# Two steps reordered on VectorE: a scaling in a band attention, and the joining of rotated pairs in an attention weave

## The reference

```
def apply_rotary(x, cos, sin):
    x1, x2 = jnp.split(x, 2, axis=-1)
    return jnp.concatenate([x1 * c - x2 * s, x1 * s + x2 * c], axis=-1)
...
b_out = moba_attention(rot(mq), rot(mk), heads(mv))
```

```
m = jnp.maximum(jnp.max(scores, axis=-1, keepdims=True), sink_b)
e = jnp.exp(scores - m)
probs = e / (jnp.sum(e, axis=-1, keepdims=True) + jnp.exp(sink_b - m))
out = jnp.einsum('bnhgqk,bnkhd->bnqhgd', probs.astype(v.dtype), vb)
```

## Time and profile before

| | |
|---|---|
| time, median of 3 runs | 2084.06 us (2082.97 to 2089.34) |
| the profiled execution | 2090.52 us, span 2088.5 us |
| PE busy | 2051.5 us, 98% of the span |
| PE weight loads busy | 1383.0 us, 66% |
| DVE busy | 987.6 us, 47% |
| ACT busy | 546.9 us, 26% |
| POOL busy | 29.6 us, 1% |
| chain that ended last | PE 89%, DVE 4%, ACT 4%, issue 2%, DMA 1% |

### The profile page before, as it was taken

The page is one execution under the profiler, slowest core; times in us unless marked ns, Lnnn a source line. Parts: engine busy times, 40 slices in busy tenths (PEclk is TensorE's granted clock), DMA queues, the critical chain, the costliest instruction groups (busy, mean ns, idle before and its releaser), DMA issues.

```text
span 2088.5 us, 23656 instructions
## 1 busy us (share of the span) xinstructions
PE 2051.5 (98%) x9752; PEld 1383.0 (66%) x9752; DVE 987.6 (47%) x1457; ACT 546.9 (26%) x1078; POOL 29.6 (1%) x16
## 2 busy tenths in 40 slices
PE   9999999999999999999999999999999999999998
PEld 5677565876888777786678888868754444333357
DVE  3776544556655454674566657644541101101145
ACT  4745352320001232203222435330140000000024
POOL 0121000000000000000000000000000000000000
PEclk9999999999999999999999999999999999999999
DMA  8311111322222120223221211312659999999961
GB/s 212 81 41 49 57 58 41 81 101 78 84 81 91 46 76 31 81 81 68 85 81 41 81 41 41 81 52 81 242 206 397 416 405 419 420 419 420 419 240 41
DMA packets 117978, 316.79 MB, mean 152 GB/s; under 512 B 38064, under 2 KB 46384, under 8 KB 93680
## 3 DMA queue, kind: packets, MB, share of 16 engines
q1 hardware_dynamic: 115520, 313.28, 40.4%
q10 hardware_dynamic: 2352, 2.00, 0.4%
HBM read 312.83 MB, written 2.10 MB: 151 GB/s over the span
## 4 chain that ended last, share of the span: by engine, by line
PE 89%; DVE 4%; ACT 4%; issue 2%; DMA 1%; DVEq 0%; SPq 0%; ACTq 0%
PE bank L459 37%; PE bank L473 17%; PE bank L3056 10%; PE bank L3106 5%; PE bank L2970 2%; PE bank L2992 2%; PE bank L1837 2%; PE bank L1429 1%; PE bank L1407 1%; PE bank L1457 1%; PE bank L2558 1%; DMA wide<-in_w_exp_gate 1%; PE bank L2548 1%; PE bank L2984 1%; PE bank L2976 1%
## 5 line engine op out<-in xcount | busy, mean ns | idle before, releaser
L459 PE MATMUL bank<-hT,ring 128*128 128x256 f32 x1168 | 267.7, 383 | 0.5 <-ACT av L608 0.5
L459 PEld LDWEIGHTS bank<-hT,ring 128*128 128x128 f32 x1168 | 221.0, 192 | 36.2 <-issue 6.0
L473 PE MATMUL bank<-hT,ring 128*128 128x512 f32 (+1 forms) x416 | 187.4, 602 | 5.0 <-DMA ring<-in_l_w_in 5.0
L459 PE MATMUL bank<-l_quarter,l_quarter 128*128 128x256 f32 x672 | 153.8, 381 | 0.5 <-DVE rqk L1665 0.5
L473 PEld LDWEIGHTS bank<-hT,ring 128*128 128x128 f32 (+1 forms) x416 | 76.9, 190 | 96.8 <-issue 90.7
L459 PEld LDWEIGHTS bank<-l_quarter,l_quarter 128*128 128x128 f32 x672 | 126.0, 190 | 20.4 <-issue 3.0
L3056 PE MATMUL bank<-wide,xg 128*64 128x512 f32 x488 | 124.8, 595 | 0.8 <-DMA wide<-in_w_exp_gate 0.8
L3056 PE MATMUL bank<-ring,xg 128*64 128x512 f32 x352 | 100.2, 595 | 1.3 <-DMA ring<-in_w_exp_gate 1.3
L3224 DVE TENSOR_TENSOR xT<-bank,xT 128x512 f32<-128x512 f32 x32 | 22.1, 692 | 157.4 <-PE bank L2970 157.3
L3056 PEld LDWEIGHTS bank<-wide,xg 128*64 128x64 f32 x488 | 38.7, 137 | 75.2 <-issue 75.2
L459 PE MATMUL bank<-ring,hT 128*128 128x256 f32 x384 | 86.7, 381 | 0.2 <-DVE gv_hi L743 0.2
(11 more groups left out here) (573 smaller groups left out, 3357.8 us busy)
## 6 DMA issues: line engine op xcount, KB each, us to landing
wide<-in_w_exp_down SPq DMA_DIRECT2D x38, 1024.0 KB, 13.5
ring<-in_l_w_in SPq DMA_DIRECT2D x18, 2048.0 KB, 7.8
wide<-in_w_exp_gate SPq DMA_DIRECT2D x34, 1024.0 KB, 10.6
wide<-in_w_exp_up SPq DMA_DIRECT2D x27, 1024.0 KB, 14.1
ring<-in_w_exp_up SPq DMA_DIRECT2D x25, 1024.0 KB, 10.4
ring<-in_w_exp_down SPq DMA_DIRECT2D x21, 1024.0 KB, 15.1
ring<-in_w_in SPq DMA_DIRECT2D x10, 2048.0 KB, 8.4
ring<-in_w_exp_gate SPq DMA_DIRECT2D x19, 1024.0 KB, 11.7
```

Source lines behind the costliest of these rows:

```text
L459: mm = pe.matmul(self.out(n)[:, half * 256:half * 256 + 256], *halves[half][k], start=i == 0 and not job["goes_on"], stop=False, skip_grou ...
L473: mm = pe.matmul(self.out(n), *mats[i], start=i == 0, stop=i == len(mats) - 1)
```

## The change

In the weave, DVE joins the pairs of step s-2 of the table behind the maximum (and the output, if any) of step s and ahead of its reciprocal; before, it joined the pairs of step s-1 of the table behind the scaling at the end of step s. In the band, the evictions of step 2 go from ahead of the scaling of unit 1 to the head of step 2; the evictions of step 1 stay ahead of the scaling of unit 0. No instruction is added or removed, and PE, ACT, POOL and SP keep their order.

```
@@ weave, vector engine
                     if s == NU0 + 2:
                         for n in range(2):
                             out0.dense.take(dve, "dve", n)
+                    for _, r in turn_at.get(s - 2, ()):
+                        put_together(dve, r)
                     if s < NU0:
                         dve.wait_ge(a_exp, s + 1)
                         step(dve.reciprocal(rv_, tot))
...
                         dve.tensor_tensor(p, p, rv_.unsqueeze(3).to_broadcast([P, 2, nj, w]), ALU.mult).then_inc(a_scaled, 1)
-                    for _, r in turn_at.get(s - 1, ()):
-                        put_together(dve, r)
@@ band, vector engine
-                    if s == 0 or s > 2:
+                    if s != 1:
                         take_step(s)
...
                     dveq(dve.reciprocal(rv_, tot))
-                    if s < 2:
-                        take_step(s + 1)
+                    if s == 0:
+                        take_step(1)
```

## The result

| | before | changed |
|---|---|---|
| time, median of 8 runs | 2085.59 us (2082.32 to 2090.15) | 2092.18 us (2090.23 to 2093.84) |
| the profiled execution, span | 2090.52, 2088.5 | 2090.23, 2088.4 |

The ratio is 1.0025, 95% interval 1.0016 to 1.0033: 5.2 us longer, 3.3 to 6.9. The forecast was +5.4, and "no measurable change": 5.2 is clear of zero, but under the 6.3 us that the prediction took as the edge (the interval reaches over it).

A forecast was written before the change was run, and what follows sets the result against it. PE's list was taken to bound the kernel. Weave +10.5 and band -5.1 gave +5.4 us, on the 2084.1 median 2089.5 us, called no measurable change; own range 2086.5 to 2092, whole range 2082 to 2094.5.

The forecast's parts named there:

- Bound and place: Whole kernel: it ends when PE has done its list; a DVE edit counts only by PE's waiting.
- Band, removed wait: Band: PE's wait for the scaling of unit 1 goes, -3.0 us, and the slow clock behind it, -3.0 us.
- Band, added wait: Band: PE newly waits 0.9 us for the eviction of product 4, with no clock loss.
- Weave, new waits: Weave: PE waits 4.9 us for ACT's eviction near 190 and 3.9 us for exponentials before the scores of unit 16.
- Weave, what goes away: Weave: waits of 0.3, 0.5 and 1.8 us go, with 1.7 us of slow clock behind the last.
- Weave, clock: Weave: slow clock costs 3.0 us behind each of the two new waits; bounds 0 and the wait itself.
- nearest row: Weave: clock loss per new wait taken from the profiled 3.0 us wait, which lost 3.0 us.
- growing clock loss: Rival, weave: clock loss grows with the wait, 8.8 us and not 6.0; sum +8.2, 2092.3 us; chance 0.25.
- silent clock: Rival, weave: the clock does not answer to the new waits; sum -0.6, 2083.5 us; chance 0.09.
- Free swaps: Rival, weave: ACT's swaps find the join done, so both edits only help; -9.4, 2074.7 us; chance 0.07.
- Absorption: Rival, expert layers: load waits of 2.1 us swallow part of the shift; +3.3, 2087.4 us; chance 0.05.
- Anywhere between nothing and its full size: Every clock term: by the skill's free-running gate, the same wait may cost a different amount in each execution.

The follow-up runs named there:

- the joins alone: Kernel before with only the weave's joins moved, the band as before: ratio 1.0041 (1.0029 to 1.0054), +8.6 us.
- the band alone: Kernel before with only the band's evictions moved, the weave as before: ratio 0.9975 (0.9966 to 0.9983), -5.2 us.

## Why the prediction was right, and where it was off

- **Bound and place.** Right: PE's list sets the end, and both halves act through PE's waits.
- **Band, removed wait (-3.0) and clock (-3.0).** The wait is right. The clock was taken from one execution: over three of the same kernel it was 3.0, 3.0 and 0, so 2.0 on average (the joins alone, where that wait stays, lost 1.7), and the band is worth about -4.2 by rows. The time of the band alone, -5.2 (-7.1 to -3.5), agrees with either.
- **Band, added wait (+0.9, no clock).** Right: 0.76 us for line 743, full clock, and gone when product 4 is evicted first.
- **Weave, new waits (4.9 and 3.9).** Right, mechanism and size: 4.69 and 3.89. One sign was off: ACT was to idle near 10 us ahead of both swaps, and did so for tile 9 (10.05), but 7.23 ahead of tile 13; the 3.9 us had been worked out from other rows and did not rest on it. The joins of steps 12 and 16 cost nothing, as said; the kernel that moves only those shows it.
- **Weave, what goes away.** The waits did go. The reason given for the 1.8 us (joins between a scaling and the next maximum) was half of it: with four swap tiles the wait goes though the joins stay. The same holds for the 0.5.
- **Weave, clock ("3.0 for each new one, the nearest row").** This is the term that was mis-sized: 1.5 to 1.7 behind each in all three traces of the changed kernel. "Nearest row" was the wrong rule, since the loss was not set by the length of the wait.
- **Sum.** With the clock at its average over the three traces of each kernel: weave 4.7 + 3.9 + 1.6 + 1.7 - 0.3 - 0.5 - 1.8 - 1.1 = +8.2 (the joins alone measured +8.6), band -4.2, together +4.0 against +5.2 measured (3.3 to 6.9). That +5.4 came so near was luck in part: the weave's new clock was too high by 2.7, but the clocks taken off in band and weave were too high as well, by 1.0 and 0.6, and these errors have opposite signs.
- **Rivals.** The growing clock loss is refuted (4.7 us of wait lost 1.5 to 1.7, 3.0 lost up to 3.0). The silent clock is refuted for the new waits, though those of 1.8 and 3.0 us were silent in one execution. Free swaps: refuted as forecast, and made true by two more tiles, at -7.1. Absorption: the 1.6 us of the profiled pair are mostly the difference between executions, and a remainder under 1 us is not separable in the times.
- **The clock of one wait.** Behind the same wait of 3.04 us the traces lose 3.0, 3.0 and 0 us. The Trainium skill (TensorE: Matmul & The Clock Gate, What's actually happening) has a gate that is judged on a clock running free of the kernel. The traces agree in so far as one wait had different prices in different executions, and for the waits of 1.8 and 3.0 us it was the better guide than the nearest row. "Anywhere between nothing and its full size" was too wide for the two new waits: ten times measured, they lost 1.5 to 3.1. No trace shows that free clock itself.

## What to carry to other kernels

Before a step is moved behind an instruction that waits, look for who waits for the step, and on which engine that one is queued ahead of what: here the later joins by themselves held up neither DVE nor PE, but ACT's next swaps shared their buffers, and an eviction stood behind the swaps. Move the steps that nobody awaits, or add a buffer: with the band's change in all three, both gave 7 us where the whole move cost 5. In the weave alone that is a gain of about 2 us in place of a loss of 8.6. When a change is worth a few us, price the clock behind a wait from several executions, and look at a pair of profiles place by place, since their totals can cancel. A slow stretch costs time only where PE is what everything waits for.

## What the runs showed of the hardware that I had not expected

- The same wait of PE, 3.04 us, was followed by 3.0 us of lost clock in two executions of the kernel before and by none in a third; the three took 2090.52, 2089.39 and 2083.57 us. The first two also lost 3.4 us each near 101, the third nothing: the clock accounts for most of this kernel's spread.
- The wait of 0.76 us in the band was never followed by a slow stretch, but a short wait is not always free: near 1520 the clock fell in four of fourteen traces behind a wait of 0.71 us and short matmuls (lines 2998 to 3008), at a cost of at most 1.2 us in the time. At about 101 us the clock fell in five of the six traces of the two kernels though PE's last wait was 0.34 us; ahead of it stand many short matmuls of 32 columns (line 1415). What brings it down there was not tried.
